# The order of ScalarE's and VectorE's work in the first four steps of a fused FFN

## The reference

```python
h = rmsnorm(x, ffn_norm)
g = jnp.einsum('bsd,df->bsf', h, w_gate)      # 1024 x 2816
u = jnp.einsum('bsd,df->bsf', h, w_up)
x = x + jnp.einsum('bsf,fd->bsd', jax.nn.silu(g) * u, w_down)   # 2816 x 1024
return rmsnorm(x, final_norm)
```

## Time and profile before

| | |
|---|---|
| median of 3 runs | 294.99 us (294.31 to 295.48) |
| profiled execution | 295.97 us, span 294.1 us |
| granted TensorE clock, mean | 0.995 |
| TensorE busy | 284.9 us (97%) |
| VectorE busy | 263.4 us (90%) |
| ScalarE busy | 190.0 us (65%) |
| chain that ended last | TensorE 80%, VectorE 5%, DMA 5%, ScalarE 3% |

### The profile page before, as it was taken

How to read it: one execution, slowest core, us unless ns; L and a number is a source line. 1 busy time by engine, 2 the same in 40 slices (tenths; PEclk the granted TensorE clock), 3 DMA queues, 4 the chain that set the end, 5 groups by cost and what they waited for, 6 DMA issues and landing times.

```text
span 294.1 us, 4124 instructions
## 1 busy us (share of the span) xinstructions
PE 284.9 (97%) x1396; PEld 231.8 (79%) x1396; DVE 263.4 (90%) x422; ACT 190.0 (65%) x323; POOL 24.7 (8%) x30
## 2 busy tenths in 40 slices
PE   8999999999999999999999999999999999999990
PEld 4778888888788788888877888888888888888880
DVE  3888999998898869798899999999999999987984
ACT  4877668755796529849566574748484857664624
POOL 0001000000122504300000000000000000000063
PEclk9999999999999999999999999999999999999997
DMA  7999617798868827695676678685748391313003
GB/s 247 381 421 380 214 40 230 217 291 248 240 192 193 313 95 264 196 300 183 176 288 213 255 220 315 198 338 157 308 121 344 96 356 52 143 36 144 2 0 143
DMA packets 29653, 62.87 MB, mean 214 GB/s; under 512 B 3648, under 2 KB 16960, under 8 KB 28224
## 3 DMA queue, kind: packets, MB, share of 16 engines
q1 hardware_dynamic: 27616, 61.04, 61.1%
q10 hardware_dynamic: 2016, 1.57, 1.7%
HBM read 55.72 MB, written 1.11 MB: 193 GB/s over the span
## 4 chain that ended last, share of the span: by engine, by line
PE 80%; DVE 5%; DMA 5%; ACT 3%; SPq 2%; issue 2%; POOL 1%; POOLq 0%; ACTq 0%
PE bank L596 26%; PE bank L598 25%; PE bank L597 25%; DMA room<-in_first 3%; DMA room<-room 2%; PE bank L673 2%; SPq L503 1%; PE bank L623 1%; PE bank L646 1%; SPq L474 1%; DVE o_lo L1439 1%; PE bank L606 1%; ACT x_hi L942 1%; ACT o_hi L1093 1%; POOL rot L1649 1%
## 5 line engine op out<-in xcount | busy, mean ns | idle before, releaser
L596 PE MATMUL bank<-w_hi,x_hi 128*128 128x512 f32 x224 | 88.9, 397 | 0.8 <-ACT room L1055 0.6
L598 PE MATMUL bank<-w_hi,x_lo 128*128 128x512 f32 x224 | 87.3, 390 | 0.0
L597 PE MATMUL bank<-w_lo,x_hi 128*128 128x512 f32 x224 | 87.3, 390 | 0.0
L596 PEld LDWEIGHTS bank<-w_hi,x_hi 128*128 128x128 f32 x224 | 42.1, 188 | 11.2 <-ACT room L1055 1.0
L598 PEld LDWEIGHTS bank<-w_hi,x_lo 128*128 128x128 f32 x224 | 42.0, 188 | 8.9
L597 PEld LDWEIGHTS bank<-w_lo,x_hi 128*128 128x128 f32 x224 | 42.1, 188 | 8.2
L910 ACT ACTIVATE w_hi<-raw 128x1024 fp32r<-128x1024 f32 x33 | 33.7, 1049 | 10.4 <-issue 9.9
L1217 DVE TENSOR_TENSOR w_lo<-raw,w_hi 128x1024 fp32r<-128x1024 f32 x32 | 38.3, 1211 | 1.8 <-ACT w_hi L910 1.7
L1376 DVE TENSOR_TENSOR w_lo<-raw,w_hi 128x1024 fp32r<-128x1024 f32 x30 | 36.2, 1217 | 1.2 <-ACT w_hi L1043 0.9
L1043 ACT ACTIVATE w_hi<-raw 128x1024 fp32r<-128x1024 f32 x29 | 30.2, 1052 | 0.0
L1054 ACT ACTIVATE rope_b<-bank,rstd 128x256 f32<-128x256 f32 x22 | 10.3, 470 | 28.5 <-PE bank L598 28.3
(11 more groups left out here) (151 smaller groups left out, 500.9 us busy)
## 6 DMA issues: line engine op xcount, KB each, us to landing
raw<-in_weights SPq DMA_DIRECT2D x74, 512.0 KB, 5.5
room<-in_weights SPq DMA_DIRECT2D x10, 1024.0 KB, 6.8
room<-room SPq DMA_DIRECT2D x76, 64.0 KB, 2.1
room<-in_first SPq DMA_DIRECT2D x1, 1024.0 KB, 8.4
xs<-in_x SPq DMA_DIRECT2D x2, 512.0 KB, 10.0
rot<-turned_sums SPq DMA_DIRECT2D x8, 128.0 KB, 3.9
room<-in_first SPq DMA_DIRECT2D x2, 384.0 KB, 5.1
room<-room ACTq DMA_DIRECT2D x12, 64.0 KB, 2.7
```

Source lines behind the costliest of these rows:

```text
L596: pe.matmul(dst, a_hi, w1, start=first, stop=False)
L597: pe.matmul(dst, a_hi, w2, start=False, stop=False)
L598: return pe.matmul(dst, a_lo, w1, start=False, stop=last)
```

## The change

On ScalarE, in the lists: `gate_up_hi(2, 0)` goes ahead of `evacuate(0, 1)`; `hidden_hi(0)` goes behind `gate_up_hi(2, 3)` and `down_first_hi(0, 1)`; `down_second_hi(0)` goes ahead of `hidden_hi(1)` and `hidden_sums_hi(1)`. In `step(3)` alone, `evacuate(3, 0)` and `hidden_hi(2)` change places around `gate_up_hi(4, 2)`. On VectorE: `gate_up_lo(2, 0)` goes ahead of the second half's multiply and turn of chunk 0; `multiply(2, 0)` ahead of `hidden_sums(1)`; `down_second_lo(0)` ahead of `turn_squares(2, 0)` and `hidden_lo(1)`; in `step(3)` alone, `hidden_sums(2)` goes behind `gate_up_lo(4, 2)` and `multiply(3, 0)`. No instruction is added or removed, and no wait changes. SP's and TensorE's lists stay as they are.

```diff
@@ ScalarE, chunks 0 to 2
             evacuate(0, 0)
+            gate_up_hi(2, 0)
             evacuate(0, 1)
             act.dma_start(gain_out, final_norm.partition_broadcast(P)).then_inc(in_gout, 16)
-            gate_up_hi(2, 0)
             gate_up_hi(2, 1)
             down_first_hi(0, 0)
             gate_up_hi(2, 2)
-            hidden_hi(0)
             gate_up_hi(2, 3)
             down_first_hi(0, 1)
+            hidden_hi(0)
             evacuate(1, 0)
...
             evacuate(2, 0)
+            down_second_hi(0)
             hidden_hi(1)
             hidden_sums_hi(1)
-            down_second_hi(0)
             gate_up_hi(3, 3)
@@ ScalarE, step(c)
-                hidden_hi(c - 1)
+                if c > 3:
+                    hidden_hi(c - 1)
+                else:
+                    evacuate(c, 0)
                 if c < NCH - 1:
                     gate_up_hi(c + 1, 2)
                 else:
                     last_down_hi(1)
-                evacuate(c, 0)
+                if c > 3:
+                    evacuate(c, 0)
+                else:
+                    hidden_hi(c - 1)
                 hidden_sums_hi(c - 1)
@@ VectorE, chunks 0 to 2
-            for s in range(SH):
-                multiply(0, s)
-                turn_squares(0, s)
+            multiply(0, 0)
+            turn_squares(0, 0)
             gate_up_lo(2, 0)
+            multiply(0, 1)
+            turn_squares(0, 1)
             gate_up_lo(2, 1)
...
             gate_up_lo(3, 2)
+            multiply(2, 0)
             hidden_sums(1)
-            multiply(2, 0)
+            down_second_lo(0)
             turn_squares(2, 0)
             hidden_lo(1)
-            down_second_lo(0)
             gate_up_lo(3, 3)
@@ VectorE, step(c)
                 gate_up_lo(c + 1, 1)
-                hidden_sums(c - 1)
+                if c > 3:
+                    hidden_sums(c - 1)
                 gate_up_lo(c + 1, 2)
                 multiply(c, 0)
+                if c == 3:
+                    hidden_sums(c - 1)
                 turn_squares(c, 0)
                 hidden_lo(c - 1)
```

## The result

The changed kernel takes 295.85 us (median of 15, 295.14 to 296.34) against 295.07 (15 runs, 294.31 to 296.07): ratio 1.0023, 95% interval 1.0012 to 1.0034. By the ratio that is 0.7 us slower, where 0.3 faster was forecast.

What follows compares the result with a forecast made beforehand. TensorE, busy for 97% of the span, was taken as the bound. From 294.99 us, stall A (-0.79), stall B (-0.82) and new stall C (+1.29) gave -0.32, so 294.7 us, range 293.9 to 295.5.

Steps and rivals of the forecast that it cites:

- the sum: Total of the three stall terms, -0.79 -0.82 +1.29 = -0.32 us, subtracted from the median to give 294.7.
- Stall B: TensorE's wait ahead of the second half of `gate_up(3)`: 0.82 us, removed by the earlier eviction in step 3.
- Stall A: TensorE's wait ahead of `down_second(0)`: 0.79 us, removed by putting `down_second_hi(0)` ahead of `hidden_hi(1)`.
- Stall C: New TensorE wait ahead of `down_second(1)`, near 163.4: 1.18 us plus 0.11 for the restart, +1.29.
- The chain of step 3: From TensorE's end of the half through ScalarE and VectorE to `down_second_lo(1)`, ending at 164.55; VectorE waits 0.5.
- VectorE's gain of 0.88 in chunk 0: VectorE's 0.88 us wait at 133.37 goes, so SP sends the squares of chunk 1 at 138.55, not 139.43.
- no new wait after step 3: Later steps keep their order, with 0.7 us to spare at `down_second_lo(2)`, so nothing comes back there.
- The slower one: Rival: a late down block delays `down_sums(1)`, up to 296.46 us; chance of some 0.13, of the slower verdict 0.04.
- The interleaving rule: Transfers from different engines share 16 DMA engines, so the gain load's 0.95 us shift could delay the squares to 134.2.

Runs made afterwards that it cites:

- e1: The kernel before once more, with no edit: ratio 1.0007.
- e3: The kernel before with only `hidden_sums(2)` moved behind `gate_up_lo(4,2)` and `multiply(3,0)` on VectorE: 296.56 us, ratio 1.0050.
- e5: The kernel before with the 512 KB final gain load on SP's queue, directly ahead of the squares of chunk 0: 295.35 us, ratio 1.0000.
- e7: The kernel before with the final gain load issued later on ScalarE, behind `gate_up_hi(3,1)`: 294.90 us, ratio 0.9989.
- e9: The kernel before with SP sending the squares of chunk 0 only after `gate_up_lo(2,0)`: 295.67 us, ratio 1.0010.
- e10: The kernel before with SP sending the squares of chunk 0 only after `gate_up_lo(2,1)`: 297.05 us, ratio 1.0045.
- e2: The changed kernel with `hidden_sums(2)` kept ahead of `gate_up_lo(4,2)` on VectorE in step 3: 294.69 us, ratio 0.9986.
- e6: The changed kernel with the 512 KB final gain load on SP's queue, directly ahead of the squares of chunk 0: 295.67 us, ratio 1.0011.
- e12: The kernel before with the step 3 moves of both engines alone: 296.28 us, ratio 1.0020.
- e4: The changed kernel with step 3 put back as before on both engines: 295.10 us, ratio 1.0000.

## Why the prediction was wrong

*The step that failed is the sum.* "I carry the difference over": the working was made on one execution of before, which took 295.97 us, 0.98 above its median, and the gain was subtracted from the median as if the stalls were in it. That 0.98 was a warning that the text named and then set aside: with only 1.61 us of stalls at stake, the difference between that execution and a usual one was more than half of the stake. Against the five other profiles in which ScalarE and VectorE work in the order of before up to B (e1, e3, e5, e7, e9; e10, whose squares were made late, is left out), these terms were mis-sized:

- Stall A, -0.79: it grows only when the squares of chunk 0 land more than about 7.7 us after the end of chunk 0. In the five they landed at 7.63 to 7.80 and A cost 0.04 to 0.19, 0.09 in the mean. The text used that landing, "I take 4.7, as before", beside a median of 2.1, and asked only what a late landing would do to the new order, never what an early one would do to the old.
- Stall B, -0.82: 0.57 to 0.67 in the five, 0.60 in the mean. It ends on the squares of chunk 2, but their transfer is steady: they landed 4.04 us after their issue in the profile shown (153.18 to 157.22) and 4.05 in e1. In the profile shown they were sent 29.73 us after the end of chunk 0 instead of 28.76, 0.97 later, with TensorE only 0.79 later by A. So most of B comes in every run, and its excess followed from the late squares of chunk 0.
- Stall C, +1.29: measured 1.36. Its chain doesn't begin at a transfer but at TensorE's own end of the half, so it comes in every run.

-0.09 - 0.60 + 1.36 = +0.67, against 295.07 x 0.0023 = +0.68 measured. Of the 1.61 us to be won, 0.92 hung on a transfer's luck, about as much as that execution lay above the median of the 15 (295.97 - 295.07 = 0.90); the 0.69 that is there in a usual run was traded for a loss of 1.36. That the profile of the changed kernel came out 0.30 under the one of before, as forecast, holds for that unusual execution alone.

*What was right.* The chain of step 3, link by link, with VectorE's wait at `gate_up_lo(4,2)` (0.76 instead of 0.5) and its end within 0.05 us; the removal of A and B; VectorE's gain of 0.88 in chunk 0 (the squares of chunk 1 left at 139.20 - 0.70 = 138.50, predicted 138.55); no new wait after step 3. One reading was off without harm: the squares of chunk 0 left 1.35 us later, as predicted, but landed at 132.91 - 0.70 = 132.21, not at 133.2. The step from C to its cure was not taken: the text says that "the new order puts `multiply(3,0)` and ScalarE's wait for TensorE into it", and the sums could have stayed where they were. e2 shows that this costs nothing and is worth 1.1 us.

*The rivals.* The slower one named the wrong place: the down block landed in time, and `down_sums(1)` started without a wait. The interleaving rule of the Trainium skill (DMA: Bandwidth & Descriptors, section Issuing engines are not separate DMA queues) was weighed for the gain load. In the order of before, neither moving the load 12 us away (e7) nor putting it ahead of the squares (e5) moved their landing by more than 0.2 us: no cost of it shows there. In the new order the squares landed at 9.73 with the load ahead of them (e6), 1.0 to 2.1 us later than in the three profiles without (8.76, 8.16 and 7.66), and only 0.42 of that is their later issue. So there a cost by that rule is not excluded.

*What stays open.* Why the squares landed 0.8 us later in the profile shown of before. It is not their own issue, which was 1.81 us after the end of chunk 0 both times (125.26 - 123.45), and the gain load stands at the same place in both. The weight pairs sent ahead of them were not varied. In the 5 us up to 2 us after the end of chunk 0 the DMA engines moved 203 GB/s in the profile shown, 239 in e1 and 277 in e12, whose squares landed soonest of the three, but 208 in e3 (7.70): slower transfers ahead of the squares fit, but are not shown. How often such a landing comes in unprofiled executions can't be read off; that the measured difference agrees with the usual values says that it is not the rule.

## What to carry to other kernels

Before counting a stall as winnable, ask whether it ends on a transfer, and whether the profiled execution sits at the median: if it took longer by as much as the stall is worth, take a second profile or price the stall at zero as one end. A and B both end on a transfer, and only the second profile told the one that comes seldom from the one that comes each time. An order that waits for a late transfer elsewhere is insurance; it must not be paid for with a wait in every run. When an item is moved ahead of another, look at what the moved engine was waiting for at that place: work that filled a wait should stay in it (`hidden_sums(2)` in front of `gate_up_lo(4,2)`).

## What the runs showed of the hardware

- Four 64 KB transfers sent 1.26 us later landed no later (e9: 7.71 against 7.63 after the end of chunk 0), and sent 2.4 us later they landed 1.6 later (e10). In e9 and e10 they took 4.6 and 5.1 us from the first issue to `hidden_hi(0)`, in e1 5.8. That the early ones waited for the 512 KB loads sent before them would explain it; no run shows it.
- The landing varies with the order of work unchanged. Sent 1.80 or 1.81 us after the end of chunk 0, these transfers landed at 6.96 (e12) to 8.42 (profile shown); sent at 3.16 or 3.17, at 7.66 (e2), 8.16 (e4) and 8.76 (changed). In those last three SP's queue took 2.95, 3.46 and 4.05 us for the four issues themselves, against 2.5 us for those of chunk 1 in all three.
- Profiles of kernels that are alike up to there differ by up to 1.3 us at the end of chunk 0 (123.22 in e7 to 124.53 in e10): more than the whole effect looked for. Comparing profiles from that point on took this out.
- TensorE's restart after a stall cost 0.11 us beyond the stall: the first matmul took 0.50 us instead of 0.39 and the next one started 0.34 after it instead of 0.23, after a gap that lost 0.21 us (e4) as after one that lost 1.50 (e10). The granted clock stayed 1.00 through stall C (160 to 170 us of the changed kernel).
